# Seven block products instead of eight for the first layer's attention projections

## Chip, core and metric

One core of one Trainium2 chip. The time is the device time of one execution in microseconds; the median of the runs counts. All matrix work is fp32.

## What is computed

Two blocks after each other on 512 latent tokens (D = 1024) and 256 context tokens. The change is in the first block's first layer: both kinds of tokens are normed, modulated and projected, attended by three mixers of eight heads each (A: global, grouped keys, normed queries and keys, rotated; B: two-dimensional neighbourhood; C: window with a sink logit, rotated), gated with a silu and projected back.

```python
hx = rmsnorm(x, norm_w) * (1 + scale) + shift      # 512 tokens
hc = rmsnorm(cx, norm_w) * (1 + scale_c) + shift_c # 256 tokens
px = split_cols(hx @ w_in)    # qA kA vA qB kB vB qC kC vC gates
pc = split_cols(hc @ w_in)
ya, yca = global_gqa(...); yb, ycb = neighbourhood_attn(...); yc_, ycc = window_gqa(...)
ux = concatenate([ya, yb, yc_]) * silu(px[9])
x = x + gate * (ux @ w_out)
```

The second layer, then a block with a recurrent and a Hyena mixer, a convolution and two mixtures of 16 experts follow; they make up the time from 1457 us on (the second layer from 830) and the change leaves them as they are, but for where the second layer's weighted values go.

## The kernel before

Everything is kept transposed: features on the 128 partitions, tokens along the free dimension. HT (8 tiles of 128 features x 768 tokens) holds the normed input, XC the residual. Weights arrive in units of 1 MB in a ring of four slots (W), loaded by SyncE's queue as they come free. GpSimd only issues DMAs: rows for the modulation vectors (in_mod_rows) and the biases of the B heads, in an order sorted by step.

Attention runs in 12 pairs of heads, B0 to B3, A0 to A3, C0 to C3; a pair has six query tiles of 128 tokens in the first layer (four latent, two context), so 72 steps. schedule() writes one order of items, and every engine walks the same list and picks what is its own. A step n is: S (scores of the next tile into BIG), T (transposes of this tile's probabilities into PT, two banks), mod (modulation sums on VectorE, one or two), T2 (the rest of T for over eight tiles), E (exponentials of the next tile on ScalarE, maximum and scaling on VectorE), then projections of the next pair as filler, then O (weighted values). VectorE takes O's result, multiplies by the gate (SG) and writes U.

The projections of pair i lie in the steps of pair i - 1. inserted() lists them: "mm" items for keys, queries, values and gates, each output tile in two parts (512 and 256 tokens) of eight matmuls, summed in one of two PSUM banks PJ that are used in turn (next_pj); ScalarE copies keys, queries and (B) values out of it, and takes tanh of the gates straight from it (L1645), after which VectorE combines tanh and gate, again from PJ (L2049). For A and C values are made by tokens ("vt", 48 matmuls of 128 columns, once for A and once for C since four pairs share keys). In B the values are transposed after that ("v_tokens", L994) and copied by VectorE (L2177). norm_ (A) has a square, a sum over the partitions on TensorE, logarithm and exponential on ScalarE (L1672, L1676) and a multiplication on VectorE (L2065); rope_ (A, C) has a matmul (L1014) and three operations of VectorE (L2075 to L2079). O writes the PJ bank that isn't the current one, so it waits for that bank's reader. Where a step has no filler two matmuls are issued to keep the clock ("clock").

The output projection (720 to 830 us) already goes by seven block products (PRODUCTS, outputs_from_products), with sums of weights and tokens on VectorE.

Lines: L804 is the helper mm of all projections, L1042 to L1053 are S, L1068 is T, L1089 is O, L1692 the exponentials, L1703 the copies of PT, L1992 the modulation sums, L2092 and L2094 the scaling, L2190 and L2206 bias and maximum.

Of the kernel before, what the change touches and what calls it, by code (L numbers as in the profile page):

```python
# [17 lines left out]
P = 128  # L18
D = 1024
KT = D // P  # L20
# [73 lines left out]

def inserted(layer, i):


    kind, j = PAIRS[i]
# [29 lines left out]
def weight(item):  # L128

    what = item[0]  # L130
    if what == "mm":
        return 2 if item[3] == 0 else 1
    return {"vt": 0.5, "v_tokens": 2.5, "norm_k": 3, "norm_q": 3, "rope_k": 2, "rope_q": 2}[what]


def late_transposes(layer, i, t):
# [3 lines left out]
    return 2 * keys > 8  # L140


def schedule(layer):
# [6 lines left out]
    for i in range(1, len(PAIRS)):  # L150
        todo = inserted(layer, i)
# [11 lines left out]
    if layer == 0:  # L163
        order.insert(order.index(("mm", 0, "q", 0, 0)), ("vectors", 0))
    for n in range(-1, last + 1):
# [7 lines left out]
        if n >= 0 and late_transposes(layer, *steps[n]):  # L173
            if todo and todo[0][0] == "mm" and todo[0][4] < KT - 1 or todo and todo[0][0] == "vt":
                order.append(todo.pop(0))
# [16 lines left out]
def unit_order():  # L192

    first = [("ada", 0, u) for u in range(MOD_UNITS * FIRST_STEPS)]
    for layer in range(DEPTH):
        u = 0
        for item in schedule(layer)[1]:
            if item[0] == "mm" and item[2] in ("k", "q") and item[3:] == (0, 0):
# [17 lines left out]
class Count:  # L216
# [4 lines left out]
    def __init__(self):  # L221
        self.big = self.pt = self.units = 0
# [23 lines left out]
    def next_unit(self):  # L246
        self.units += 1
        return self.units - 1
# [5 lines left out]

    def next_o(self):

        return self.use_pj(1 - self.pj_bank)
# [32 lines left out]
def build(nc, A):  # L290
# [15 lines left out]
    with ExitStack() as ctx:  # L306
# [205 lines left out]
        gate_tanh = sem("gate_tanh")  # L512
        pj_filled = sem("pj_filled")
# [11 lines left out]
        o_filled = sem("o_filled")  # L525
        hidden_filled = sem("hidden_filled")
# [49 lines left out]
        out_stored = sem("out_stored")  # L576

# [161 lines left out]
        def _(pool):  # L739
# [29 lines left out]

            load_mod_vectors(0)  # L770
# [6 lines left out]
            jobs.append((mod_step(MODS_DONE[1] - 1), 2, 0))  # L777
            for _, what, x in sorted(jobs):
                if what == 0:
# [17 lines left out]
        def _(pe):  # L797
# [144 lines left out]
            def attention(layer):  # L942
# [4 lines left out]
                outputs, before_last = [0, 0], None  # L947
                if layer:
                    me.next("probs_exp", 2)
                kv = -1  # L950
                use = None
                for item in order:
                    what, x = item[0], item[1]
                    if what == "mm":
# [15 lines left out]
                        if k == KT - 1:  # L970
# [4 lines left out]
                            if which in ("v", "g") and b == (NA if which == "v" else nq):  # L975
                                unit_done()
                    elif what == "vt":
# [10 lines left out]
                    elif what == "v_tokens":  # L988
                        pe.wait_ge(pj_free[raw_use["v", x][0]], raw_use["v", x][1] + 1)
                        for tiles in (range(4), (4, 5, 6)):  # L990
                            use = next_pj()
                            for t in tiles:
                                token = NEAR_FROM[t] if t in NEAR_FROM else t * P
                                last = pe.transpose(PJ[use[0]][:, t % 4 * P:t % 4 * P + P],  # L994
                                                    SQT[:, token:token + P], const("ident"))
# [59 lines left out]
                    elif what in ("T", "T2"):  # L1055
                        i, t = steps[x]
                        tiles = prob_tiles(PAIRS[i][0], t)
                        for n, (h, y) in enumerate(tiles):
# [4 lines left out]
                            if n % 4 == 0:  # L1063
                                unit_at = me.next_unit()
                                if unit_at >= 2:
                                    pe.wait_ge(t_copied, unit_at - 1)
                            a = unit_at % 2 * 512 + n % 4 * P
# [4 lines left out]
                    elif what == "O":  # L1072
# [4 lines left out]
                        use_o = me.next_o()  # L1077
# [1730 lines left out]
```

## Time and profile before

| | us |
|---|---|
| runs | 3037.84, 3032.97, 3027.95 |
| median | 3032.97 |
| profiled execution, whole | 3034.02 |
| its span in the trace | 3032.2 |
| first layer's attention, steps of all pairs | 45 to 720 |
| its output projection | 720 to 830 |
| TensorE busy in the span | 2894.1 |
| VectorE busy | 1291.7 |
| ScalarE busy | 748.6 |
| GpSimd busy | 82.8 |

Times in the trace are microseconds from the span's start. A row of a timeline gives start, length, engine, line, operation and, in brackets, how long the engine idled before it and whose work ended that.

### The profile page before, as it was taken

The page shows a single profiled execution, that of the slowest core. Times are in us where ns is not written, and L with a number is a line of the kernel's source. Part 1 is how long each engine was busy: PE and PEld are TensorE (multiplying, and loading weights), DVE is VectorE, ACT ScalarE, POOL GpSimd, SP SyncE. Part 2 cuts the span into 40 slices and gives each one's busy share as a digit, 9 for nine tenths or more (in the row PEclk, how much of TensorE's full clock was granted, in tenths as well). Part 3 has the DMA queues.
Part 4 walks back from the last instruction along what each step waited for, and adds up shares of the span by engine and source line. Part 5 has one row for each costly group of instructions (what it writes and reads, how often), then busy time and mean ns, then how long its engine had stood idle before and what let it go on. Part 6 is the DMA issues. An engine that isn't in the chain of part 4 may idle for free.

```text
span 3032.2 us, 33976 instructions
## 1 busy us (share of the span) xinstructions
PE 2894.1 (95%) x13444; PEld 1538.4 (51%) x13444; DVE 1291.7 (43%) x2511; ACT 748.6 (25%) x1338; POOL 82.8 (3%) x156
## 2 busy tenths in 40 slices
PE   7999989999999999989999999999999998999998
PEld 3556656665555655558544545444443434444442
DVE  1455665787335466684466742111112533111112
ACT  3223455342122354340352111000002122000001
POOL 0000000000000000010000000000000000000000
PEclk9999999999999999999999999999999999999999
DMA  6222221223113233332111038999994225999997
GB/s 270 80 87 73 80 92 62 87 81 112 74 59 139 96 118 101 122 131 106 66 64 42 27 120 330 409 421 422 422 420 200 83 83 228 409 421 421 422 421 295
DMA packets 90526, 583.44 MB, mean 192 GB/s; under 512 B 10176, under 2 KB 10176, under 8 KB 29216
## 3 DMA queue, kind: packets, MB, share of 16 engines
q1 hardware_dynamic: 69696, 502.56, 41.3%
q0 software_dynamic: 20704, 79.11, 7.8%
q8 instruction: 90, 1.47, 0.2%
q14 instruction: 36, 0.29, 0.0%
HBM read 579.53 MB, written 2.10 MB: 192 GB/s over the span
## 4 chain that ended last, share of the span: by engine, by line
PE 86%; DVE 9%; ACT 3%; issue 1%; DMA 1%; SPq 0%; DVEq 0%; ACTq 0%
PE BIG L804 46%; PE PJ L804 20%; PE BIG L1535 4%; PE PT L1068 3%; PE PJ L1089 3%; PE BIG L1049 2%; PE BIG L1053 2%; PE PT L804 1%; DVE SPILL L1992 1%; PE PJ L853 1%; DVE STAT L2206 1%; ACT ARENA L1692 1%; PE BIG L1042 1%; PE PT L1511 1%; DMA W<-in_units 0%
## 5 line engine op out<-in xcount | busy, mean ns | idle before, releaser
L804 PE MATMUL PJ<-HT,W 128*128 128x512 f32 (+1 forms) x1792 | 649.8, 513 | 11.4 <-ACT ARENA L1672 6.3
L804 PE MATMUL BIG<-ARENA 128*64 128x512 f32 (+3 forms) x2656 | 550.5, 459 | 4.8 <-DVE ARENA L2508 2.5
L804 PEld LDWEIGHTS PJ<-HT,W 128*128 128x128 f32 x1792 | 332.2, 192 | 250.1 <-issue 217.9
L804 PEld LDWEIGHTS BIG<-ARENA 128*128 128x128 f32 (+1 forms) x2656 | 289.7, 167 | 252.4 <-issue 222.8
L804 PE MATMUL BIG<-HT,W 128*128 128x512 f32 (+1 forms) x768 | 320.0, 577 | 2.4 <-DVE ARENA L2343 2.1
L804 PE MATMUL BIG<-W,ARENA 128*64 128x512 f32 (+1 forms) x1280 | 282.0, 573 | 0.9 <-DVE ARENA L2389 0.9
L1703 ACT ACTIVATE ARENA<-PT 128x512 f32<-128x512 f32 (+1 forms) x264 | 144.4, 583 | 468.4 <-PE PT L1068 467.6
L2537 DVE SCALAR_TENSOR_TENSOR XC<-BIG,MOD,XC 128x512 f32<-128x512 f32 x128 | 90.2, 747 | 377.9 <-PE BIG L1535 377.9
L804 PEld LDWEIGHTS BIG<-HT,W 128*128 128x128 f32 x768 | 146.5, 191 | 172.9 <-issue 165.7
L1992 DVE CUSTOM_DVE_ANT_0 SPILL<-W,VEC 128x1024 bf16<-128x1024 f32 x168 | 214.8, 1278 | 11.2 <-issue 4.5
L2206 DVE TENSOR_REDUCE STAT<-BIG 128x1 f32<-128x512 f32 (+5 forms) x240 | 170.0, 725 | 46.8 <-PE BIG L1053 41.9
L804 PEld LDWEIGHTS BIG<-W,ARENA 128*64 128x64 f32 (+1 forms) x1280 | 107.4, 142 | 161.0 <-issue 154.8
L1692 ACT ACTIVATE ARENA<-BIG,STAT 128x512 f32<-128x512 f32 (+5 forms) x240 | 170.9, 717 | 21.5 <-DVE STAT L2206 20.7
L804 PE MATMUL BIG<-HT,ARENA 128*64 128x512 f32 x576 | 169.7, 592 | 0.0
L1089 PEld LDWEIGHTS PJ<-ARENA 128*64 128x64 f32 x2048 | 110.4, 136 | 92.8 <-issue 51.4
L1089 PE MATMUL PJ<-ARENA 128*64 128x128 f32 x2048 | 139.3, 278 | 18.2 <-DVE ARENA L2049 11.7
L1068 PE MATMUL PT<-CONST,ARENA 128*128 128x128 f32 x1024 | 148.6, 281 | 6.0 <-DVE ARENA L2094 4.3
L1068 PEld LDWEIGHTS PT<-CONST,ARENA 128*128 128x128 f32 x1024 | 111.8, 141 | 66.7 <-issue 44.1
L804 PE MATMUL BIG<-ARENA,W 128*128 128x512 f32 (+2 forms) x384 | 136.5, 513 | 0.1
L2094 DVE TENSOR_SCALAR ARENA<-ARENA,STAT 128x512 f32<-128x512 f32 (+3 forms) x240 | 121.6, 506 | 8.5
L2101 DVE SCALAR_TENSOR_TENSOR ARENA<-PJ,ARENA 128x128 f32<-128x128 f32 x120 | 37.4, 312 | 192.2 <-PE PJ L1089 191.7
L1535 PE MATMUL BIG<-ARENA 128*128 128x512 f32 x256 | 115.0, 602 | 0.0
(282 smaller groups left out, 2352.1 us busy)
## 6 DMA issues: line engine op xcount, KB each, us to landing
ARENA<-in_exp_w SPq DMA_DIRECT2D x168, 1024.0 KB, 18.1
W<-in_exp_w SPq DMA_DIRECT2D x144, 1024.0 KB, 16.8
W<-in_units SPq DMA_DIRECT2D x89, 1024.0 KB, 5.0
HT<-in_exp_w SPq DMA_DIRECT2D x72, 1024.0 KB, 22.0
W<-in_mod_rows POOLq DMA_DIRECT2D x128, 512.0 KB, 3.9
ARENA<-in_bias_b POOLq DMA_DIRECT2D x16, 384.0 KB, 5.5
XC<-in_x SPq DMA_DIRECT2D x1, 3072.0 KB, 11.2
W<-in_mod_vectors POOLq DMA_DIRECT2D x2, 1024.0 KB, 7.9
```

The source lines that it names most:

```text
L804: ins = pe.matmul(out, lhsT, rhs, start=start, stop=stop, skip_group_check=skip)
L1049: pe.matmul(BIG[h][:, N - (b - a) * P:N], Q[rows, i % 2, t * P:t * P + P], keys[rows, a * P:b * P], start=True, stop=True)
L1053: pe.matmul(BIG[h][:, N:NA], Q[rows, i % 2, t * P:t * P + P], keys[rows, N:NA], start=True, stop=True).then_inc(scores_filled, 1)
L1068: last = pe.transpose(PT[:, a:a + P], PROB[:, h, y * P:y * P + P], const("ident"))
L1089: last = pe.matmul(PJ[use_o[0]][head * HD:head * HD + HD, 0:P], V[:, buf_of[i], tile, head * HD:head * HD + HD], PTS[:, at:at + P], start= ...
L1535: last = pe.matmul(BIG[k_use % 2][:, half * N:half * N + N], YK[:, m * P:m * P + P], GSCAT[:, :], start=True, stop=True)
L1692: act.activation(PROB[:, h, 0:b - a], BIG[h][:, a:b], ACT.Exp, bias=STAT[:, c:c + 1], accum_out=STAT[:, 4 + c:5 + c]).then_inc(probs_exp, 1)
L1703: act.activation(PTS[:, a:a + w], PT[:, bank:bank + w], ACT.Copy).then_inc(t_copied, 1)
L1992: dve.tensor_tensor_reduce(SPILL[:, :], MODW[:, row % 2, :], MODV[:, which, :], 1.0, vec("mod_b", at), ALU.mult, ALU.add, MOD[:, at:at + 1 ...
L2094: dve.tensor_scalar(probs, probs, STAT[:, 8 + c:9 + c], None, ALU.mult)\
L2206: dve.tensor_reduce(STAT[:, c:c + 1], out[:, a:b], AX.X, ALU.max, negate=True).then_inc(max_ready, 1)
L2537: ins = dve.scalar_tensor_tensor(XC[:, m, 0:N], BIG[k_use % 2][:, half * N:half * N + N], mod(group, 5, m, 0), XC[:, m, 0:N], ALU.mult, AL ...
```

## The change

In the first layer all projections but the first pair's keys and values go in units of two output tiles (keys and values, or queries and gates) over all 768 tokens, by seven products of 2 x 2 blocks: features in halves of four tiles, tokens in halves of 384, the two output tiles as the other halves. A product is four matmuls of 384 columns into a PJ bank. Products 6, 7 and 4 go on adding in the bank of products 1, 6 and 7 (X), product 3 in that of product 5; products 1, 6, 5 and 4 are copied from there by ScalarE into their destination and products 2, 7 and 3 are added to it by VectorE.

- Four sums of weight blocks per unit are made on GpSimd, one in place over a block of the loaded weights; before each it waits for the unit's load and for the last product that reads the sum before. Four differences of token blocks are made once, on VectorE, in XC, and x is loaded into XC again behind the last unit.
- The gate is copied raw into SG, tanh goes over all 768 tokens at once from SG, and VectorE combines them in SG ("tanh", "gate" items).
- Values of A and C come out as features by tokens like those of B and are transposed ("v_tokens").
- The order of the items is new (inserted_by_blocks, block_slots): the "next" item puts what follows a step later; in the A and C pairs the last step's filler is the next unit's first product.
- Weighted values (O) go, in both layers, to the PT bank of the last transposes instead of a PJ bank, with a semaphore of their own (o_read) that the next transposes into that bank wait for.

Two steps where B0 ends and B1 begins, from the new schedule (P are products; x is a count of matmuls):

```
S5(B0 t5) | T 4 | mod 6 | mod 7 | E 5 | qg P3 x3 | qg P4 x4 | tanh 1 | O 4
S6(B1 t0) | T 5 | mod 8 | E 6 | gate 1 | v_tokens 1 | kv P1 x4 | kv P2 x4 | kv P6 x2 | O 5
```

The diff, cut to its core:

```diff
+BLOCK_PRODUCTS = [1, 2, 6, 5, 7, 3, 4]
+BLOCK_K = KT // 2
+BLOCK_N = NA // 2
+def inserted_by_blocks(i):
+    kind, j = PAIRS[i]
+    out = []
+    if i == 0:
+        out += [("mm", i, what, part, k) for what in ("k", "v") for part in range(2) for k in range(KT)]
+    elif kind == "B":
+        out += by_blocks(i, "kv")
+    elif kind == "A" and j == 0:
+        out += by_blocks(i, "kv", 0, 6) + [("square", i, "k")] + by_blocks(i, "kv", 6)
+        out += [("v_tokens", i), ("norm_k", i)]
+    elif j == 0:
+        out += by_blocks(i, "kv") + [("v_tokens", i)]
+    if kind == "A":
+        out += by_blocks(i, "qg", 0, 6) + [("square", i, "q")] + by_blocks(i, "qg", 6) + [("norm_q", i)]
+    else:
+        out += by_blocks(i, "qg")
+    out.append(("tanh", i))
+    if i == 0:
+        return out + [("v_tokens", i), ("gate", i)]
+    if j == 0 and kind != "B":
+        out.append(("rope_k", i))
+    return out + [("next", i)] + ([("gate", i), ("v_tokens", i)] if kind == "B" else [("rope_q", i), ("gate", i)])
...
+            def add_weights(u):
+                n, (a11, a12, a21, a22) = weights_of(u)
+                pool.wait_ge(unit_loaded[n % RING], 16 * (n // RING + 1))
+                if u:
+                    pool.wait_ge(pj_filled, uses[u - 1][3][0])
...
+                pool.tensor_tensor(ADDED[:, 0], a21, a22, ALU.add).then_inc(weights_added, 1)
+                pool.wait_ge(weights_added, 4 * u + 1)
+                pool.tensor_tensor(ADDED[:, 1], ADDED[:, 0], a11, ALU.add).then_inc(weights_added, 1)
+                pool.tensor_tensor(a21, a21, a11, ALU.add).then_inc(weights_added, 1)
+            def add_last_weights(u):
...
+                pool.tensor_tensor(ADDED[:, 2], ADDED[:, 1], a12, ALU.add).then_inc(weights_added, 1)
...
+                    pool.wait_ge(pj_filled, uses[-1][6][0])
+                    pool.dma_start(XC[:, :, :], A["x0"]).then_inc(x_again, 16)
...
+                        product = BLOCK_PRODUCTS[position]
+                        if k == 0:
+                            use = next_pj()
+                            if product in (6, 7, 3):
+                                pe.wait_ge(weights_added, 4 * block_unit + {6: 2, 7: 3, 3: 4}[product])
...
+                        last = mm(PJ[use[0]][:, 0:BLOCK_N], lhsT, rhs, k == 0 and product in (1, 2, 5),
+                                  k == BLOCK_K - 1, skip=product in (6, 7, 3, 4))
...
+                                if output_in[unit_at % 2]:
+                                    pe.wait_ge(o_read, output_in[unit_at % 2])
...
-                        use_o = me.next_o()
-                        if use_o[1]:
-                            pe.wait_ge(pj_free[use_o[0]], use_o[1])
...
+                        bank = (units_through[x] - 1) % 2
...
-                                last = pe.matmul(PJ[use_o[0]][head * HD:head * HD + HD, 0:P],
+                                last = pe.matmul(PT[head * HD:head * HD + HD, bank * 512:bank * 512 + P],
...
+                        act.wait_ge(pj_filled, use[2])
+                        scale = -1.0 if tile else block_scale(i, which)
+                        for out, src in block_parts(i, of, dst, PJ[use[0]], half):
+                            ins = act.activation(out, src, ACT.Copy, scale=scale)
+                        ins.then_inc(pj_free[use[0]], 1)
...
+                        if product in (2, 7):
+                            dve.wait_ge(pj_free[before[0]], before[1] + 1)
+                        dve.wait_ge(pj_filled, use[2])
+                        scale = -1.0 if tile else block_scale(i, which)
+                        for out, src in block_parts(i, of, dst, PJ[use[0]], half):
+                            ins = dve.scalar_tensor_tensor(out, src, scale, out, ALU.mult, ALU.add)
+                        ins.then_inc(pj_free[use[0]], 1)
+                    elif what == "gate":
+                        dve.wait_ge(gate_tanh, me.next("gate_tanh"))
+                        dve.scalar_tensor_tensor(SG[:, x % 2, :], GATE_T, 1.0, SG[:, x % 2, :],
+                                                 ALU.add, ALU.mult).then_inc(gated, 1)
```

## Rows read from the trace of the kernel before

**Rows 1.** The page's part 1: busy time, share, instructions.
```profile
PE 2894.1 (95%) x13444; PEld 1538.4 (51%) x13444; DVE 1291.7 (43%) x2511; ACT 748.6 (25%) x1338; POOL 82.8 (3%) x156
```

**Rows 2.** Busy time by stretch: engines' busy us (instructions), clock, DMA share, GB/s.
```profile
103.00:285.00 182.00, 176.08 (x894) 108.98 (x894) 94.03 (x214) 50.35 (x126) 10.20 (x19) 0.99 0.25 86
285.00:352.00 67.00, 63.14 (x384) 42.95 (x381) 38.03 (x79) 25.49 (x52) 3.26 (x6) 1.00 0.22 75
352.00:500.00 148.00, 134.33 (x817) 82.11 (x815) 90.17 (x184) 87.36 (x156) 8.79 (x16) 1.00 0.25 82
500.00:560.00 60.00, 58.17 (x389) 42.05 (x389) 31.55 (x66) 17.38 (x40) 2.15 (x4) 1.00 0.17 53
560.00:683.00 123.00, 118.51 (x717) 73.71 (x716) 103.32 (x269) 49.93 (x123) 7.43 (x14) 1.00 0.27 86
```

**Rows 3.** TensorE's waits from 45 to 720 us: total, times, longest.
```profile
PE BIG L1049 <- DVE ARENA L2079: 8.4, 7, 1.4
PE PJ L804 <- ACT ARENA L1672: 6.7, 4, 1.8
PE PJ L994 <- DVE ARENA L2049: 5.1, 4, 2.1
PE BIG L1042 <- DVE ARENA L2049: 2.2, 4, 1.0
```

**Rows 4.** The chain that ended last, pieces: start, us, what (512, 384, 256, 128 columns).
```profile
1770.85 6.87 PE PT L804 x16
725.13 23.46 PE BIG L804 x72
1368.90 15.54 PE BIG L804 x72
309.30 9.20 PE PJ L804 x80
```

**Rows 5.** Timeline of the step S6 (B1's first scores): TensorE's transposes, VectorE's chain.
```profile
155.42 0.66 PE L1068 MATMUL PT<-CONST,ARENA 128*128 128x128 f32 x4
155.50 0.43 DVE L2190 TENSOR_TENSOR BIG<-BIG,ARENA 128x256 f32<-128x256 f32 x1 [1.05 <-PE BIG L1053]
157.63 1.27 DVE L1992 CUSTOM_DVE_ANT_0 SPILL<-W,VEC 128x1024 bf16<-128x1024 f32 x1
159.62 0.49 DVE L2094 TENSOR_SCALAR ARENA<-ARENA,STAT 128x512 f32<-128x512 f32 x1
```

**Rows 6.** Timeline of VectorE: two value copies, a product over 768 columns.
```profile
86.83 1.28 DVE L2177 COPY ARENA<-PJ 128x512 f32<-128x512 f32 x2
387.20 1.02 DVE L2065 SCALAR_TENSOR_TENSOR ARENA<-ARENA,VEC 128x768 f32<-128x768 f32 x1 [3.15 <-ACT ARENA L1676]
```

**Rows 7.** Busy time by stretches of 4 us, columns as in rows 2.
```profile
144.00:148.00 4.00, 1.80 (x10) 0.85 (x8) 3.85 (x11) 1.20 (x5) 0.54 (x1) 1.00 0.13 28
148.00:152.00 4.00, 4.00 (x11) 3.23 (x12) 0.50 (x1) 0.00 (x0) 0.00 (x0) 0.57 0.27 103
2436.00:2440.00 4.00, 0.52 (x2) 0.00 (x0) 3.75 (x8) 0.00 (x0) 0.00 (x0) 0.86 1.01 426
2440.00:2444.00 4.00, 3.69 (x5) 1.62 (x6) 1.40 (x3) 0.42 (x1) 0.00 (x0) 0.50 0.11 45
```

**Rows 8.** Timeline of ScalarE in A0's last step: logarithm, exponential and their table loads.
```profile
382.66 1.28 ACT L1672 ACT_TABLE_LOAD   x1
385.03 1.28 ACT L1676 ACT_TABLE_LOAD   x1
387.19 1.28 ACT L1678 ACT_TABLE_LOAD   x1
```

**Rows 9.** Timeline around S54 (C1's first scores): VectorE's rotation, TensorE.
```profile
592.15 0.66 PE L1068 MATMUL PT<-CONST,ARENA 128*128 128x128 f32 x4
598.20 0.69 DVE L2079 TENSOR_TENSOR ARENA<-ARENA 128x512 f32<-128x512 f32 x1
```

**Rows 10.** TensorE's waits from 830 to 1365 us, the second layer.
```profile
PE PJ L1089 <- DVE ARENA L2049: 11.7, 8, 2.2
```

More of the change, by code:

```diff
@@ L92, in mod_step, with by_blocks, block_slots @@
     return late + x * (sum(STEPS) - SECOND_VECTORS - 1) // len(MOD_OPS)
+BLOCK_PRODUCTS = [1, 2, 6, 5, 7, 3, 4]
+BLOCK_K = KT // 2
+BLOCK_N = NA // 2
+def by_blocks(i, which, first=0, end=len(BLOCK_PRODUCTS)):
+    return [("block", i, which, position, k) for position in range(first, end) for k in range(BLOCK_K)]
+def inserted_by_blocks(i):
[20 more added lines that the diff above has]
+    return out + [("next", i)] + ([("gate", i), ("v_tokens", i)] if kind == "B" else [("rope_q", i), ("gate", i)])
+def block_slots(i, tiles):
+    todo = inserted_by_blocks(i)
+    early = BLOCK_K if PAIRS[i - 1][0] != "B" else 0
+    room = tiles if PAIRS[i][0] == "B" else tiles - 1
+    total, done, least, before = sum(weight(x) for x in todo[early:]), 0, 0, 0
+    out = [(-1, item) for item in todo[:early]]
+    for item in todo[early:]:
+        at = max(min(int(done * room / total), room - 1), least)
+        done += weight(item)
+        if item[0] == "next":
+            least = before + 1
+            continue
+        out.append((at, item))
+        before = at
+    return out
 def inserted(layer, i):
+    if layer == 0:
+        return inserted_by_blocks(i)
     kind, j = PAIRS[i]
@@ L132, in weight @@
         return 2 if item[3] == 0 else 1
-    return {"vt": 0.5, "v_tokens": 2.5, "norm_k": 3, "norm_q": 3, "rope_k": 2, "rope_q": 2}[what]
+    return {"block": 1.5, "square": 0, "tanh": 0, "gate": 0, "next": 0, "vt": 0.5, "v_tokens": 2.5, "norm_k": 3, "norm_q": 3, "rope_k": 2, "rope_q": 2}[what]
 def late_transposes(layer, i, t):
@@ L150, in schedule @@
     for i in range(1, len(PAIRS)):
+        if layer == 0:
+            for at, item in block_slots(i, tiles):
+                slots[(i - 1) * tiles - 1 + at].append(item)
+            continue
         todo = inserted(layer, i)
@@ L1092, in attention @@
                         last.then_inc(o_filled, 1)
-                for bank in range(2):
-                    pe.wait_ge(pj_free[bank], before_last[bank])
+                pe.wait_ge(o_read, steps_before + len(steps) - nq // P)
                 n = nq // 2
@@ L2036, in attention @@
                 kv = -1
+                use = None
+                if layer == 0:
+                    block_tokens()
                 for item in order:
@@ L2081, in attention @@
                         modulation(x)
+                    elif what in ("T", "T2"):
+                        columns = len(prob_tiles(PAIRS[steps[x][0]][0], steps[x][1])) * P
+                        me.next_unit(len([a for a in range(0, columns, 512) if (a < 1024) == (what == "T")]))
                     elif what == "S":
```

230 lines of the change are left out of this document (200 added, 30 removed).

## The prediction

> **What bounds the kernel now.** I read the page's totals first, then the busy time by stretch, then TensorE's waits, then the timelines of single steps. TensorE is busy 2894 of 3032 us, VectorE 1292 [rows 1]: time goes away only where TensorE's own work shrinks, and comes back wherever TensorE waits. The change touches the first layer's attention, 45 to 720 us. There TensorE works all but 6 us of 182 in the B pairs, 14 of 148 in the A pairs, 4.5 of 123 in the C pairs; but in C VectorE too is busy 103 of 123 [rows 2]. What TensorE waits for is a few hand-overs: rotated queries (L2079, 8.4 us), the norm's logarithm (L1672, 6.7), the gate's read before the value transposes (L2049, 5.1) [rows 3].
>
> **What a matmul costs.** Each fp32 matmul of the program is two rows of the trace (the x16 of a run of eight). Back to back one of 512 columns takes 6.87/8 = 0.86 us, of 384 23.46/36 = 0.65, of 256 15.54/36 = 0.43, and a value product of 128 columns 9.20/40 = 0.23 [rows 4]: proportional to columns down to 256.
>
> **The gain, on the path.** A unit (two output tiles over 768 tokens) is now 16 x 0.86 + 16 x 0.43 = 20.6 us; as seven products of four matmuls of 384 it is 28 x 0.645 = 18.06. Fifteen units gain 2.58 each: 38.7. The k/v units of A0 and C0 are now 10.3 + 48 x 0.23 = 21.4 and become 18.06 plus six transposes (four take 0.66 with their tail [rows 5], so about 0.8): 2.5 each, 5.0. Sum 43.7 us. The first k/v unit stays.
>
> **What it costs, step by step.** Two banks (PJ) now turn over every 2.6 us instead of 3.4 or more, and each product is read before the next but one may start. I walked each pair's order of steps with the durations of the rows: ScalarE's read comes behind the copies of the probabilities and the two exponentials, 2.2 to 2.7 us after the transposes end; VectorE's read behind the maximum, the modulation sums and the scaling, 4 us after them with one modulation sum, 5.3 with two. Most products are long enough to hide that. These aren't:
>
> (a) B1 to B3: the new order puts gate, then the two value copies, ahead of the next unit's first product, which uses the bank of the first copy. VectorE in that step: bias and maximum from 155.50, a modulation sum at 157.63, scaling until 160.11 [rows 5]. Behind that come the gate over 768 columns (1.02, by a norm's product of that size) and one copy (0.64) [rows 6]: the bank is free at 161.9. TensorE ends its four transposes at about 156.0 [rows 5] and seven value transposes at 156.9: it idles 5.0 us, and 6.4 in the two pairs with two modulation sums (1.35 more each). 17.8 us, in place of 5.3 of waits that go (most of L994's 5.1 and a part of L1042's 2.2 [rows 3]): 12.5. One product of B3's unit waits for VectorE's read behind two modulation sums: 0.7.
>
> (b) TensorE's clock. In 144 to 148 the engine idles 2.2 us, and the next 4 us have a granted clock of 0.57, i.e. mostly the lower of the two levels (1.2 GHz); after 3.5 us of idling at 2436 to 2440 it is 0.50 [rows 7]. Each such fall costs about 1.7 us of work. Three stalls of (a) bring three, and one of today goes: 3.4.
>
> (c) A0's own projections (in B3's steps): values wait for ScalarE's read (1.35), the norm for the value copy (1.1), a product for VectorE's read behind two modulation sums (2.6), the first scores of A0 for query rotation behind key rotation, maximum and two modulation sums (4.4), small ones 0.6: 10.1, against about 3.8 today (one wait each for the logarithm, the norm and the rotation, of those of rows 3), and two falls of the clock: 9.7.
>
> (d) A1 to A3: a gain. Today logarithm, exponential and tanh need table loads of 1.28 us, three of them in 6 us [rows 8], with TensorE waiting at both ends; with Tanh once after the norm the table loaded behind the square serves both, and norm and rotation are a step apart. I get 2.5 us of waits per pair against 4.5: -6.
>
> (e) C0's projections: 4.0 of waits against 1.0, one clock fall: 4.7.
>
> (f) C1 to C3: each step's rotation ends VectorE's chain 6.1 us after the transposes, whatever TensorE does [rows 9]: TensorE, with 0.86 us less work there, waits that longer (in the last pair 3.4). VectorE also gets three reads of about 0.55 and a gate of 1.02 per unit for gate reads of 0.68 and 0.42: 1.6 more, in a stretch where it is busy a third of 103, so 34.4 of 41 [rows 2]. Of 7.7 us saved I leave 1.5: 6.2.
>
> (g) The first unit: today's waits of 2.0 around its values shrink to 0.4: -1.6. Block sums of tokens are four VectorE operations of 1536 columns, 4 x 2.05 by the 1.35 ns a column of L2079 [rows 9]: 8.2 us, needed 20 us later, where VectorE has nothing else. Without that cover they would cost up to 8.
>
> (h) Weighted values go to PT: the wait of O for a PJ bank goes, also in the second layer, where it is 11.7 us [rows 10]. But next on TensorE are scores that need the rotation behind the same gate read, so it turns into that wait: -1, between 0 and -10.
>
> (i) The 68 weight sums on GpSimd. No row has one. By VectorE's 0.69 for 512 columns [rows 9] I take 0.7 as the lower end and 2.8 (four times that) as the upper. Four sums are at most 11 us per unit, with 12.9 us of products between the last use of a sum and its next: hidden, also the modulation rows' DMAs queued behind them on GpSimd, of which at least one is loaded ahead. What they do to VectorE: 0 to 40 us (below); I take 3, near the low end, since VectorE waits in more than half of the steps.
>
> (j) x is loaded again into XC (3 MB, 11 us at the start of the kernel) at about 660 us, needed at 720: nothing.
>
> Sum of costs: 12.5 + 0.7 + 3.4 + 9.7 - 6 + 4.7 + 6.2 - 1.6 - 1 + 3 = 31.6. Gain 43.7 - 31.6 = 12.1. The profiled execution took 3034.0 (span 3032.2), the median of three is 3033.0: forecast 3022.
>
> **The rule weighed.** What the rows show: VectorE's modulation sum, gate, norm and rotation read two SBUF operands each, and no row has GpSimd computing beside them. The Trainium skill, "SBUF — State Buffer", section "Who interferes with whom", says that a VectorE instruction with two SBUF inputs and a GpSimd one that reads SBUF exclude each other for the whole instruction. No row shows it. "GPSIMD Engine Reference", section 3.1, gives 2.6 cycles an element for such a sum, by which 512 elements would be an estimated 1.1 us and 68 of them 75 us, of which the shares of rival 2 would put an estimated 30 on the path.
>
> **The rivals.**
> Rival 1, the waits are smaller: if ScalarE and VectorE are as far ahead as in most steps of today, (a) is half, (c) and (e) don't grow and C keeps half its gain: 12.5 + 3.4 + 9.7 + 4.7 + 6.2 = 36.5 becomes 15, time 3000. For it: TensorE's present waits are only 38 us of 675. Against: the order of (a) is plain in the code.
> Rival 2, slower: GpSimd's sums hold VectorE up. Price: a sum of 0.7 to 2.8 us, 12 of them in C1 to C3 where VectorE is the bound, 16 in A0 and C0, 28 in units ahead of the gate and copies of (a). At 1.4 us, with all of the first, half of the second and a quarter of the third on the path: 17 + 11 + 10 = 38 in place of my 3: time 3057; it turns slower than before from about 0.5 us a sum on the path. For it: C's 84% VectorE. Against: 95 us of sums are a seventh of the stretch, and most operations of VectorE meet none.
> The rule of the Trainium skill's page "SBUF — State Buffer" is what rival 2 would rest on.
> Rival 3, the same: no contention, but C gains nothing, the clock falls at every new stall including the 2 us ones in C (six more, 1.7 each): 3022 + 1.5 + 10 = 3034.
> Rival 4, the products don't replace the work as said (a sum late for its product, so that TensorE waits for GpSimd in every unit, 2 us each): 3056.
>
> **How the numbers follow.** Forecast case (3012 to 3033) 0.48; rival 1 0.20; rival 2 0.15; rival 3 0.14; rival 4 0.03. A measurement of this kernel tells 0.3% (9 us) from no change. The forecast's case is split by that bound at 3023.9: 0.28 faster, 0.20 the same. Faster 0.48, same 0.20 + 0.14 = 0.34, slower 0.18. The range takes in rival 1 and half of rival 2: 2999 to 3048.
>
> **What would show it.** Right: PJ products with 384 columns at 0.645; a wait of L994's successor, the first product of B2, B3 and A0, for the value copy (L2177), 5 to 6.4 us, three times, with a granted clock of 0.5 behind it; a wait of A0's first scores for the rotation near 4 us; the waits for the logarithm in A1 to A3 gone; C pairs of 39 to 40 us instead of 41. Wrong: products waiting for GpSimd; VectorE operations of two SBUF operands longer or with gaps while GpSimd is busy; B pairs (60.5 us now) shorter than 58 or longer than 64.

## The result

| | before | after |
|---|---|---|
| median of 20 runs each, us | 3036.7 | 3039.2 |
| lowest to highest, us | 3028.0 to 3038.3 | 3036.1 to 3042.6 |
| ratio | 1 | 1.0016, 95% interval 1.0010 to 1.0022 |
| profiled execution: span, us | 3032.2 | 3040.8 |
| TensorE / VectorE / GpSimd busy, us | 2894 / 1292 / 83 | 2872 / 1343 / 176 |

The change makes the kernel slower by 5 us (0.16%), inside the 0.3% that counts as the same; forecast was 11 to 12 us less. The profiled execution of the changed kernel is the slowest of its 20 (3042.6), that of before lies under its median (3034.0), so the pair of traces is 8.6 us apart where the medians stand 2.5 and the ratio 4.9. The accounts below are made between the two traces, so up to some 4 us of their 8.6 are owed to which executions were traced. What differs between executions of one kernel is the granted clock: 31 executions of the kernel before run from 3027.7 us at a mean clock of 0.992 to 3039.0 at 0.988, and the 20 of the changed kernel from 3036.1 at 0.982 to 3042.6, the traced one, at 0.980.

TensorE's busy time by stretch, from its first projection to C3's first scores, first before, then after. Columns: stretch, length, busy us of TensorE, its weight loads, VectorE, ScalarE, GpSimd (instructions), granted clock, DMA share, GB/s. The borders are the first scores of B0, A0, A3, C0 and C3, as each trace has them, so that a wait for a pair's first scores counts in the stretch before.

```profile
44.30:92.83 48.53, 45.35 (x144) 26.29 (x145) 10.31 (x20) 16.96 (x27) 3.41 (x7) 0.95 0.32 125
92.83:342.86 250.03, 240.25 (x1270) 152.43 (x1269) 130.12 (x291) 75.06 (x176) 13.45 (x25) 0.99 0.24 83
342.86:491.54 148.68, 135.01 (x836) 82.99 (x834) 93.09 (x188) 83.48 (x153) 8.79 (x16) 1.00 0.25 82
491.54:558.33 66.79, 64.96 (x406) 44.87 (x404) 33.89 (x68) 24.14 (x47) 2.15 (x4) 1.00 0.20 64
558.33:680.30 121.97, 117.48 (x717) 73.54 (x716) 102.34 (x265) 48.97 (x120) 7.43 (x14) 1.00 0.27 87
```

```profile
44.30:88.47 44.17, 43.65 (x135) 25.07 (x137) 19.85 (x24) 17.04 (x28) 16.04 (x13) 0.93 0.32 124
88.47:348.79 260.32, 232.92 (x1155) 141.32 (x1153) 150.06 (x322) 80.19 (x192) 53.36 (x57) 0.94 0.25 83
348.79:483.99 135.20, 128.18 (x813) 79.28 (x811) 102.90 (x194) 73.47 (x147) 26.60 (x28) 0.99 0.28 90
483.99:556.55 72.56, 64.94 (x332) 39.30 (x330) 36.24 (x73) 25.85 (x50) 11.61 (x12) 0.93 0.14 47
556.55:688.33 131.78, 109.04 (x684) 67.98 (x683) 111.09 (x273) 51.29 (x122) 20.69 (x23) 0.96 0.30 103
```

What to see: 4.4 us go at the start, 10.3 come in B0 to B3, 13.5 go in A0 to A2, 5.8 come in A3, 9.8 come in C0 to C2. Where time comes in, two things changed beside the work: TensorE's idle part (27 of 260 us in B against 10 of 250) and its granted clock (0.93 to 0.96 against 0.99 to 1.00). From 720 us on both traces are the same but for the second layer's waits, which keep their sum.

TensorE's waits from 45 to 720 us, to be held against [rows 3] (total, times, longest):

```profile
PE BIG L1263 <- DVE ARENA L2373: 24.0, 8, 14.0
PE PJ L976 <- DVE ARENA L2477: 18.8, 4, 6.5
PE PJ L976 <- DVE ARENA L2344: 7.6, 4, 3.9
PE PT L1285 <- ACT ARENA L1959: 6.4, 12, 1.3
PE PJ L1208 <- ACT ARENA L1898: 3.4, 2, 2.2
```

L1263 are the first scores of a pair behind the rotation L2373, L976 the products behind the value copies (L2477) or VectorE's read (L2344), L1285 transposes, L1208 value transposes. In the same way L2391 below is VectorE's scaling of the probabilities and L2246 a modulation sum. The waits for the logarithm and the gate's read of [rows 3] are gone. One wait of 14.0 us stands at C3's first scores. The trace tells whose it is, in GpSimd's queue and on VectorE:

```profile
669.89 0.53 POOL L950 DMA_DIRECT2D XC<-in_x  x1 [10.53 <-PE PJ L976]
670.41 1.14 POOL L885 DMA_DIRECT2D W<-in_mod_rows  x2
...
683.12 1.28 DVE L2246 CUSTOM_DVE_ANT_0 SPILL<-W,VEC 128x1024 bf16<-128x1024 f32 x1 [10.50 <-DMA W<-in_mod_rows]
...
687.32 1.23 PE L1263 MATMUL BIG<-ARENA 64*128 64x256 f32 x4 [14.00 <-DVE ARENA L2373]
```

The reload of x (3 MB) is issued just ahead of the rows of the next two modulation sums. VectorE stands 10.5 us for those rows, and behind that sum come the scaling and the rotation that C3 needs.

### The profile page after: what moved, and what is told of

Read it like the earlier page. It is cut to its first block, busy times and chain, and to the rows that moved or that the text cites. A ratio compares the mean times of both kernels' runs of the same rounds, so it can differ in the third digit from the quotient of the medians.

```text
span 3040.8 us, 33707 instructions
## 1 busy us (share of the span) xinstructions
PE 2871.9 (94%) x13192; PEld 1513.9 (50%) x13192; DVE 1342.7 (44%) x2564; ACT 748.5 (25%) x1355; POOL 176.2 (6%) x225
## 3 DMA queue, kind: packets, MB, share of 16 engines
q8 instruction: 88, 1.44, 0.2%
## 4 chain that ended last, share of the span: by engine, by line
PE 68%; DVE 6%; ACT 1%; issue 1%; DVEq 0%; ACTq 0%
PE BIG L976 45%; PE PJ L976 9%; PE BIG L1748 4%; PE PT L1285 1%; PE PT L1302 1%; PE PT L976 1%; PE BIG L1263 1%; PE PJ L1025 1%; DVE SPILL L2246 1%; PE BIG L1267 1%; PE PT L1724 1%; DVE ARENA L2786 0%; DVE ARENA L2785 0%; PE BIG L1256 0%; PE PT L1704 0%
## 5 line engine op out<-in xcount | busy, mean ns | idle before, releaser
L976 PE MATMUL BIG<-ARENA 128*64 128x512 f32 (+3 forms) x2656 | 552.3, 461 | 4.8 <-DVE ARENA L2808 2.5
L976 PE MATMUL PJ<-HT,W 128*128 128x512 f32 (+2 forms) x1040 | 406.2, 541 | 26.2 <-DVE ARENA L2477 21.4
L976 PEld LDWEIGHTS BIG<-ARENA 128*128 128x128 f32 (+1 forms) x2656 | 290.2, 168 | 253.8 <-issue 224.2
L976 PE MATMUL BIG<-HT,W 128*128 128x512 f32 (+1 forms) x768 | 319.7, 577 | 2.4 <-DVE ARENA L2643 2.1
L976 PEld LDWEIGHTS PJ<-HT,W 128*128 128x128 f32 x1040 | 198.2, 197 | 191.1 <-issue 154.3
L976 PE MATMUL BIG<-W,ARENA 128*64 128x512 f32 (+1 forms) x1280 | 282.0, 573 | 0.9 <-DVE ARENA L2689 0.9
L976 PEld LDWEIGHTS BIG<-HT,W 128*128 128x128 f32 x768 | 146.2, 191 | 172.2 <-issue 164.8
L2246 DVE CUSTOM_DVE_ANT_0 SPILL<-W,VEC 128x1024 bf16<-128x1024 f32 x168 | 218.1, 1298 | 21.6 <-DMA W<-in_mod_rows 11.2
L976 PEld LDWEIGHTS BIG<-W,ARENA 128*64 128x64 f32 (+1 forms) x1280 | 107.4, 142 | 161.0 <-issue 154.9
L976 PE MATMUL BIG<-HT,ARENA 128*64 128x512 f32 x576 | 169.7, 592 | 0.0
L1285 PE MATMUL PT<-CONST,ARENA 128*128 128x128 f32 x1024 | 153.2, 286 | 14.1 <-ACT ARENA L1959 7.1
L1285 PEld LDWEIGHTS PT<-CONST,ARENA 128*128 128x128 f32 x1024 | 114.0, 143 | 76.8 <-issue 44.1
L1302 PEld LDWEIGHTS PT<-ARENA 128*64 128x64 f32 x2048 | 110.3, 136 | 70.5 <-issue 69.3
L2391 DVE TENSOR_SCALAR ARENA<-ARENA,STAT 128x512 f32<-128x512 f32 (+3 forms) x240 | 137.3, 572 | 8.5
L1302 PE MATMUL PT<-ARENA 128*64 128x128 f32 x2048 | 139.3, 278 | 0.0
L976 PE MATMUL BIG<-ARENA,W 128*128 128x512 f32 (+2 forms) x384 | 136.5, 513 | 0.1
L885 POOL DMA_DIRECT2D W<-in_mod_rows x128 | 69.1, 540 | 918.0 <-DVE MOD L2246 896.7
## 6 DMA issues: line engine op xcount, KB each, us to landing
XC<-in_x SPq DMA_DIRECT2D x1, 3072.0 KB, 10.1
```

Source lines behind the costliest of these rows:

```text
L885: pool.dma_start(MODW[:, x % 2, :], A["mod_rows"][x]).then_inc(mod_loaded[x % 2], 16)
L976: ins = pe.matmul(out, lhsT, rhs, start=start, stop=stop, skip_group_check=skip)
L1285: last = pe.transpose(PT[:, a:a + P], PROB[:, h, y * P:y * P + P], const("ident"))
L1302: last = pe.matmul(PT[head * HD:head * HD + HD, bank * 512:bank * 512 + P], V[:, buf_of[i], tile, head * HD:head * HD + HD], PTS[:, at:at ...
L2246: dve.tensor_tensor_reduce(SPILL[:, :], MODW[:, row % 2, :], MODV[:, which, :], 1.0, vec("mod_b", at), ALU.mult, ALU.add, MOD[:, at:at + 1 ...
L2391: dve.tensor_scalar(probs, probs, STAT[:, 8 + c:9 + c], None, ALU.mult)\
```

## The experiments

All are compared with the kernel before on the same chip. "Against the changed kernel" below is the difference of the two ratios times 3034 us; each ratio has an interval of some 0.1% to either side, so such a difference is good to 3 or 4 us; with three_mends and all_mends, of which only 5 and 4 executions were taken, to 5 or 6. Waits and clocks are from the traces and repeat to hundredths between kernels where nothing was touched (the wait for the first value copy is 5.03 or 5.04 in all six that leave it alone), so mechanisms are judged by them.

### x_on_sync and x_before_slot: another queue for the reload

```diff
-            jobs.append((uses[-1][6][1], 4, 0))
...
+            stream(A["units1"], last_block_unit + RING + 1, RING)
+            sp.wait_ge(pj_filled, block_uses()[-1][6][0])
+            sp.dma_start(XC[:, :, :], A["x0"]).then_inc(x_again, 16)
```

> The changed kernel with one edit: x is loaded again on SyncE's queue (behind the load that reuses the last unit's slot) instead of on GpSimd's, ahead of whose rows for the modulation vectors it stood. Theory: the 14.0 us wait of TensorE at C3's first scores is the queue's order (3 MB, 12 us, ahead of two rows DMAs): it falls to 3 to 5 us, and with it the low clock behind it (2.3 us lost): 10 to 13 us less than the changed kernel. Rival: the transfers share the DMA engines whatever the queue, the rows come as late: less than 4 us.

Measured: 1.0027 (1.0018 to 1.0035), nothing gained. C3's first scores wait 4.1 us, but the output products wait 12.3 for VectorE's first read into XC: the reload stood behind a load that itself waits for the first matmul of the output products, and so came late. That says nothing yet about the queues.

> The changed kernel with x loaded again on SyncE's queue, now ahead of the load that reuses the last unit's slot (that one waits for the output products' first matmul, and in x_on_sync the reload stood behind it, landed late and turned into a wait of 12.3 us there). Theory: C3's first scores wait 4.1 us as in x_on_sync instead of 14.0 and the output products wait for nothing: 10 to 12 us less than the changed kernel. Rival: on its own queue the reload slows the rows' transfers, and VectorE waits for them by 3 us or more around 675 to 685: 4 to 7 us less.

Measured: 1.0014 (1.0005 to 1.0023), 1 us less than the changed kernel. The reload is issued at 669.53 on SyncE's queue, the rows at 669.22 and 670.65 on GpSimd's. (x_before_slot puts the reload ahead of the load that it stood behind in x_on_sync, whose diff is shown.) TensorE waits 10.4 us instead of 14.0. VectorE in x_before_slot:

```profile
679.45 1.28 DVE L2246 CUSTOM_DVE_ANT_0 SPILL<-W,VEC 128x1024 bf16<-128x1024 f32 x1 [6.91 <-DMA W<-in_mod_rows]
```

Its DMA issues of 669 to 684 us (KB each, median us to landing):

```profile
XC<-in_x SPq DMA_DIRECT2D x1, 3072.0 KB, 11.4
W<-in_mod_rows POOLq DMA_DIRECT2D x3, 512.0 KB, 10.2
```

512 KB that land in 3.8 us elsewhere take 10.2 beside the 3 MB, though on a queue of their own. The theory fails, and the rival has the mechanism right: the order in one queue was 3.6 us of the wait, the sharing of the DMA engines the larger part (10.4 against the 4.1 that are left without the reload, below). The Trainium skill says this in "DMA: Bandwidth & Descriptors", section "Issuing engines are not separate DMA queues": transfers from any engine run on the same 16 engines and interleave. By that rule the trace agrees. The rival's size, 4 to 7 us less, isn't borne out: the time is 1 us less, good to 3.

### x_in_pieces: the reload between the rows

```diff
+            jobs += [(uses[-1][6][1] + 1 + k // 2, 4, k) for k in range(KT)]
...
+                    pool.dma_start(XC[:, x, :], A["x0"][:, x, :]).then_inc(x_again, 16)
```

> The changed kernel with the reload of x cut into eight DMAs of 384 KB, on GpSimd's queue as before, two in each of the four steps after the last block product, each behind the rows of its step. In x_before_slot the rows (issued 0.3 us ahead of the 3 MB and 1.1 us behind its start, on another queue) still came 6.9 us late for VectorE: not the queue's order alone but the shared transfers. Theory: rows wait for at most 3 us of other bytes, C3's first scores wait 3.5 to 4.6 us instead of 14.0: 9 to 12 us less than the changed kernel. Rival: the later rows come late in turn, one step each: 3 to 6 less.

Measured: 0.9989 (0.9980 to 0.9998), 8 us less than the changed kernel. The line of C3's first scores:

```profile
675.30 1.23 PE L1263 MATMUL BIG<-ARENA 64*128 64x256 f32 x4 [4.09 <-DVE ARENA L2373]
```

14.00 became 4.09, and the rival falls: from 650 to 745 us VectorE waits 1.2 us for rows, three times, at most 0.6, instead of 11.2. So the reload cost 9.9 us of wait; the other 4.1 are the rotation's.

### values_on_scalar: who copies the values of B

```diff
-                        values(kv, 0, me.next_pj())
...
+                                act.activation(V[:, kv % 2, a:b, :].rearrange("p a b -> p (a b)"),
+                                               PJ[use[0]][:, 0:(b - a) * P], ACT.Copy).then_inc(pj_free[use[0]], 1)
```

> The changed kernel with one edit: the two copies of the transposed values of B1 to B3 are made by ScalarE instead of VectorE. In the profile ScalarE is done with its exponentials 2.6, 4.0 and 4.0 us before VectorE's copy ends. Theory: the three waits for that copy (5.03, 6.36, 6.47 us) become 2.4 each, 10.6 us less, and with shorter stalls the clock comes back sooner, 1 to 3 us more: 11 to 14 us less than the changed kernel. Rival: VectorE is late for the next read anyway and the wait moves on to a product: 5 us or less.

Measured: 0.9973 (0.9962 to 0.9983), 13 us less than the changed kernel. The first of the three waits, in the changed kernel and here:

```profile
142.54 1.27 DVE L2246 CUSTOM_DVE_ANT_0 SPILL<-W,VEC 128x1024 bf16<-128x1024 f32 x1
...
144.93 0.95 DVE L2348 SCALAR_TENSOR_TENSOR ARENA<-ARENA 128x768 f32<-128x768 f32 x1
145.91 1.15 DVE L2477 COPY ARENA<-PJ 128x512 f32<-128x512 f32 x2
146.75 8.36 PE L976 MATMUL PJ<-HT,W 128*128 128x384 f32 x16 [5.03 <-DVE ARENA L2477]
```

```profile
142.02 0.97 ACT L1922 ACTIVATE ARENA<-PJ 128x512 f32<-128x512 f32 x2
142.75 3.06 PE L976 MATMUL PJ<-HT,W 128*128 128x384 f32 x5 [2.35 <-ACT ARENA L1922]
```

All three waits are 2.35 us (forecast 2.4), whether one or two modulation sums lie in the step: ScalarE doesn't stand behind them. The waits shrink by 10.8, the clock gives back the rest. No wait of another kind grew by more than 0.3 us.

### clock_kept: the same waits at full clock

```diff
+                            pe.wait_ge(t_copied, me.units)
+                            idle_bank({2: 5, 3: 7, 4: 7}[i], (me.units - 1) % 2)
...
+                        if layer == 0 and {24: 3, 66: 15}.get(x):
```

> The changed kernel with one addition: while TensorE waits for the value copies of B1 to B3, for A0's first scores and for C3's first scores it does matrix products of 512 columns into an idle PSUM bank (5, 7, 7, 3 and 15 of them, 0.86 us each at full clock, less than the wait they stand in). Theory: the granted clock of 0.50 behind these five waits costs 3.0, 2.1, 2.9, 1.2 and 2.3 us, 11.5 in all, and that is what goes: 8 to 12 us less than the changed kernel, with no wait shorter. Rival, that the low clock is covered by other waits or stays low: 0 to 3 us less, or more time.

Measured: 0.9985 (0.9977 to 0.9994), 9 us less than the changed kernel, with no wait made shorter by another engine. To see the clock's cost by itself I summed, over windows of 4 us from 44 to 740, TensorE's busy time times one less the granted clock: 3.8 us before, 21.8 in the changed kernel, 8.7 here. The windows behind the third value wait, in the changed kernel:

```profile
268.00:272.00 4.00, 0.00 (x0) 0.00 (x0) 3.78 (x9) 0.38 (x2) 0.55 (x1) 0.60 0.38 101
272.00:276.00 4.00, 2.87 (x5) 1.69 (x6) 1.42 (x3) 0.00 (x0) 0.00 (x0) 0.50 0.22 50
276.00:280.00 4.00, 4.00 (x9) 2.09 (x8) 0.00 (x0) 0.49 (x1) 0.00 (x0) 0.62 0.65 248
280.00:284.00 4.00, 4.00 (x14) 2.41 (x13) 0.56 (x1) 0.00 (x0) 0.00 (x0) 1.00 0.00 0
```

At 0.50, the lower level of 1.2 GHz, 2.87 us of busy time hold 1.4 us of work; this fall costs 1.44 + 1.52 = 3.0 us. The prediction had 1.7 for each. The trace of before could have told: it read the fall behind 3.5 us of idling only in the stretch 2440 to 2444 [rows 7], where it costs 1.8, and the stretch behind that one, in the kernel before, costs another 0.9:

```profile
2444.00:2448.00 4.00, 4.00 (x18) 1.45 (x17) 3.73 (x7) 4.00 (x8) 0.00 (x0) 0.78 0.00 0
```

### narrow_sums: the price of GpSimd's sums

```diff
+                n = slice(0, 1 if u else P)
+                pool.tensor_tensor(ADDED[:, 0, :, n], a21[:, :, n], a22[:, :, n], ALU.add).then_inc(weights_added, 1)
```

> The changed kernel with GpSimd's weight sums (from the second unit on) over one column of each 128 instead of all: left out is the rest of these sums, waits and order stay. It prices what GpSimd's work does to the others. Theory: VectorE's scaling of the probabilities goes back from 0.66-0.80 to 0.49-0.62 us (16 us in all over VectorE), of which a third is on the path: 3 to 7 us less than the changed kernel. Rival 2 of the prediction: some 38 us less. Rival, all of it hidden: under 2 us.

Measured: 0.9998 (0.9989 to 1.0007), 5.5 us less than the changed kernel, good to some 3. (Its trace is 9.2 us shorter, of which 2.8 are clock by the sum over windows, 19.0 instead of 21.8.) How it comes about, in A0's projections of the changed kernel (GpSimd, then VectorE), and the same two scalings with narrow sums:

```profile
289.46 1.45 POOL L919 TENSOR_TENSOR ARENA<-W 128x512 f32<-128x512 f32 x1 [19.84 <-PE PJ L976]
290.99 1.15 POOL L921 TENSOR_TENSOR ARENA<-ARENA,W 128x512 f32<-128x512 f32 x1
...
289.90 1.29 DVE L2391 TENSOR_SCALAR ARENA<-ARENA,STAT 128x512 f32<-128x512 f32 x1
291.30 1.13 DVE L2391 TENSOR_SCALAR ARENA<-ARENA,STAT 128x512 f32<-128x512 f32 x1
```

```profile
285.50 0.52 DVE L2393 TENSOR_SCALAR ARENA<-ARENA,STAT 128x512 f32<-128x512 f32 x1
286.12 0.49 DVE L2393 TENSOR_SCALAR ARENA<-ARENA,STAT 128x512 f32<-128x512 f32 x1
```

A scaling that falls on a sum ends just after it. Over the first layer (45 to 720 us) the scalings take 84.4 us in the changed kernel, 69.6 here and 69.4 before; modulation sums that begin behind a GpSimd sum take up to 2.20 us instead of 1.28, 128.7 against 127.8 in all (98 and 100 of them in the window). Reads from PSUM keep their 0.55 beside a running sum. Two instructions with two large SBUF operands each, the case of the prediction, meet too: in the first unit three of GpSimd's sums take 2.5 to 2.8 us beside VectorE's token sums, instead of 1.1 to 1.3. So the exclusion is there, and it costs VectorE some 18 us in scalings and modulation sums (14.8 in the scalings, 98 x 0.035 in the modulation sums), but only about a third of that reaches the end. The Trainium skill, "SBUF — State Buffer", section "Who interferes with whom", names this: tensor_scalar can use both port pairs of VectorE, and whichever of it and GpSimd issues first holds the shared one for the whole instruction. By that rule the trace agrees; the prediction had looked for it in instructions with two SBUF operands only, and most of the price (14.8 of 18 us) lies in scalings, which have one.

Where VectorE is the bound the price is plain: C0's steps take 40.08 us with narrow sums, 41.36 in the changed kernel and 41.15 before.

### vectors_earlier: a silu in the wrong step

```diff
-MODS_SECOND = 7 * 6 - 1
+MODS_SECOND = 7 * 6 - 2
```

> The changed kernel with the silu of the second modulation vectors (1.28 + 1.91 + 1.28 us on ScalarE with its two table loads) one step earlier than the first modulation sum that uses it. Theory: VectorE's wait of 4.49 us for it is what makes A3's product P5 wait 3.86: that goes, with 1.2 us of low clock: 4 to 5 us less than the changed kernel. Rival: ScalarE is then late for the exponentials or the read of P1 and a wait of 2 to 4 us stands a step earlier: within 1.5 us.

Measured: 1.0003 (0.9994 to 1.0012), 4 us less than the changed kernel; A3's steps go from 72.6 to 66.4 us. What stood there, in the changed kernel:

```profile
487.59 1.28 ACT L1967 ACT_TABLE_LOAD   x1
488.88 1.91 ACT L1967 ACTIVATE W<-W 128x2048 f32<-128x2048 f32 x1
490.81 1.28 ACT L1968 ACT_TABLE_LOAD   x1
...
490.92 1.28 DVE L2246 CUSTOM_DVE_ANT_0 SPILL<-W,VEC 128x1024 bf16<-128x1024 f32 x1 [4.49 <-issue]
...
494.19 4.46 PE L976 MATMUL PJ<-XC,ARENA 128*128 128x384 f32 x8 [3.86 <-DVE ARENA L2344]
```

In the kernel before VectorE waits the same 4.49 us at the same sum (at 498.48 there), and TensorE has enough projections issued not to notice. With a bank turning over every 2.6 us it does.

### mods_late: modulation sums behind the reads

```diff
+            order += [] if layer else mods
             order.append(("O", n))
```

> The changed kernel with the first layer's modulation sums moved behind the step's scaling and reads, ahead of the read of the weighted values (on VectorE; nothing else moves). It tests that 'behind one or two modulation sums' is what made the waits. Theory: the waits for value copies 5.03, 6.36, 6.47 become 3.7 each, those of products for VectorE's read (2.35 and 3.86) and A0's and C1's and C2's first scores (3.34, 2.10, 1.99) lose 1.3 to 2.6 each: 13 us, with less clock lost 15 to 18 us less than the changed kernel; the 14.0 at C3 turns into a wait of some 8 to 10 a step later. Rival: the maximum of the next step comes later by the same, and exponentials and transposes wait instead: 5 us less or none.

Measured: 1.0015 (1.0006 to 1.0023), the same as the changed kernel: a miss. The second and third value wait fall to 4.2 us, not 3.7, the first stays at 5.1, C1's and C2's rotation waits nearly go, but transposes now wait for VectorE's read of the weighted values (12.4 us in all instead of 0.8), A2's first scores wait 2.6 instead of 0.7, and the wait at C3 splits into 3.6 and 5.5. (Its traced execution is its fastest, 3033, so only waits are read from that trace.) VectorE's order isn't free to give: what a step's reads win, the next step's maximum and output read lose. The rival holds.

### outputs_in_pt: that part alone

```diff
-    if layer == 0:
-        return inserted_by_blocks(i)
```

(and with it the slots, sums and reload; the weighted values stay in PT.)

> The kernel before with one part of the change: weighted values go to PT in both layers, all projections as before. Theory (the prediction's step h): the 11.7 us wait of the second layer turns into a wait of the scores for the rotation: 0 to 2 us less than the kernel before. Rival: the wait really goes: 8 to 10 us less, and then the block products alone cost more than the comparison of the two kernels shows.

Measured: 1.0010 (1.0002 to 1.0019), 3 us more than before by the ratio; its trace is 1.4 us shorter than that of before. No gain in either, so the rival falls. The second layer's waits for the rotation are 16.3 us in 8; before they were 4.3 for the rotation and 11.7 for the bank [rows 10], together 16.0. In the first layer A0 to A2 take 1.8 us more in all and C2 0.9 less. The A pairs' waits are 14.8 us in all, as before (14.9), but gathered into fewer and longer ones: three of 2.88 us for the logarithm, where before none in these pairs was over 1.8. Behind two of the three the clock falls, 2.8 us in all, and in these pairs of the kernel before it doesn't fall at all. How the 4.9 us of the whole change are split between this part and the block products lies within the intervals and stays open.

### two_mends, three_mends, all_mends: do the causes add up

Edits: two_mends is x_before_slot with values_on_scalar; three_mends is values_on_scalar, x_in_pieces and vectors_earlier; all_mends adds matrix products into an idle PSUM bank in the waits that are left:

```diff
+CLOCK_AT = {(2, 'kv', 1): 2, (3, 'kv', 1): 2, (4, 'kv', 1): 2, (4, 'qg', 5): 2}
...
+                        if layer == 0 and {24: 3, 54: 2, 60: 2, 66: 3}.get(x):
```

> x_before_slot and values_on_scalar together. Theory: the two are independent (12.4 us less by values_on_scalar, 10 to 12 by the reload): 21 to 25 us less than the changed kernel, about 3016. Rival: VectorE in between is the common bound, the gains overlap: 14 to 18.

Measured: 0.9970 (0.9958 to 0.9981), 14 us less than the changed kernel: the sum of 13 and of the 1 that x_before_slot brings, whose own expectation had been wrong.

> values_on_scalar, x_in_pieces and vectors_earlier together. Theory: they are independent, 12.4 + 10 + 4.5 less than the changed kernel: 27, or 0.9925 to 0.9945 of the kernel before. Rival: overlap on VectorE, 0.996 to 0.998.

Measured: 0.9929 (0.9915 to 0.9943), 26 us less than the changed kernel; 13 + 8 + 4 = 25. The rival's 0.996 to 0.998 lies outside the interval: within what these ratios can tell the three causes add up.

> three_mends with matrix products into an idle PSUM bank in the waits that are left (2 of 512 columns in each of the waits of 2.35, of 2.1 and 2.0 and of 2.19 us, 3 in those of 3.3 and 3.5 to 4). Theory: the low clock behind waits of 2 to 4 us (1.3 to 2.5 us a time in the traces so far, some ten times) goes: 8 to 11 us less than three_mends. Rival: behind waits of about 2 us the clock stays up by itself in most of them: 3 to 5 us.

Measured: 0.9891 (0.9875 to 0.9906), 3001.0 us: 11.5 us less than three_mends and 33 us less than the kernel before. Summed as above the low clock takes 3.0 us of the first layer, against 15.6 in three_mends, 12.6 less, so the rival's 3 to 5 us fall; half of what is left is at the start, half behind two waits of 1.0 and 1.2 us in A0's projections that weren't filled. Two products of a unit, at full clock (16 rows are 8 matmuls):

```profile
491.14 5.40 PE L977 MATMUL PJ<-HT,W 128*128 128x384 f32 x16 [0.95 <-DVE ARENA L2504]
```

With its tail 5.40 us, by the prediction's 0.645 a matmul 5.16. The saved work is there; what the changed kernel lacked was work of other engines done in time, and TensorE's clock behind the waits for it.

## Why the prediction was wrong

Forecast was 12.1 us less, the traces show 8.6 more: 20.7 us. The 3039 us lie within the range on record, 2999 to 3048, but only since it was wide: the kernel got slower, and what was missed, steps (j), (b), (c), (e) and (i) below, all went the same way. By stretch, forecast (summed from its steps) and measured, in us. The early first products count in: the first product of each A and C unit lies one pair ahead of where it was, which puts 2.6 us into B3 and takes 2.6 from C2 without saving anything.

| stretch | forecast | measured |
|---|---|---|
| start to B0's first scores | -4.2 | -4.4 |
| B0 to B3 | +8.3 | +10.3 |
| A0 to A2 | -13.7 | -13.5 |
| A3 | -0.4 | +5.8 |
| C0 to C2 | -4.1 | +9.8 |
| C3 | 0 | +0.5 |
| sums on GpSimd (3) and O in PT (-1), not placed | +2 | in the others |

**Right.** The saved work: TensorE's busy time, less what the low clock adds to it (summed over windows of 4 us as above, here over the whole span: 22.8 us before, 41.4 after), falls from 2871.3 to 2830.5, 40.8 us of the 43.7 forecast. Step (a): idle 5.0, 6.4, 6.4 forecast, 5.03, 6.36, 6.47 measured. Step (d): the stretch A0 to A2 comes within 0.2 us; the waits for the logarithm are gone. Step (g): the start gains 4.4 us, 4.2 forecast; the token sums take 10.2 us instead of 8.2 but are hidden. Step (h): the second layer's wait turned into the rotation's, its sum unchanged (16.2 for 16.0). In (c), A0's first scores wait 3.3 (4.4 forecast), the product behind two modulation sums 2.35 (2.6), the value transposes 1.2 (1.35), the norm 1.0 (1.1); together 8.1 with the rest, of 10.1.

**Wrong, step (j), 9.9 us.** "x is loaded again ...: nothing." The transfer itself was checked against its own deadline (720 us), not against what shares the DMA engines with it. Two modulation rows are queued behind it, and C3's rotation behind the sums that need them; neither was named. x_in_pieces takes it away (14.00 to 4.09). With the clock's fall behind it, counted in the next paragraph, it cost 12 us.

**Wrong in size, steps (b), (c), (e): the clock, 9 us.** Each fall was priced 1.7 us, from single stretches of 4 us in the kernel before. Behind the three value waits it cost 2.7, 2.2 and 3.0; after A3's two waits 1.2 and 2.9; three falls instead of two in A0's projections, 4.2 in all; and C3's wait brought one of 2.3 that follows from (j). In all 21.8 us where the forecast comes to 12.3 (3.8 of today and 3.4 + 3.4 + 1.7 of the steps). The 1.7 came from a short wait, of 2.15 us: behind the three of 2.35 us in values_on_scalar the falls cost 1.3, 1.5 and 1.4. Over all traces with the waits of 5.0 to 6.5 us unfilled they cost 1.1 to 3.0 behind them, 2.3 on average, so the changed kernel's trace, its slowest execution, stands in the upper part of that. After waits of 2.0 and 2.1 us (C1, C2) the clock fell in some traces (the C1 steps take 42.98 us in x_on_sync) and not in others (41.29 in the changed kernel). That executions of one kernel differ by their mean clock is on record (0.992 to 0.988 over the kernel before's 11 us); in which places they differ isn't, since one execution of each was traced.

**Wrong, step (e), 3 us.** Waits of 7.0 us for C0's projections instead of 4.0. Among them are the 3.86 that vectors_earlier takes away, and no step of the prediction names their cause: the silu of the second modulation vectors stands in A3's first step, and VectorE's modulation sum there begins only after a wait of 4.49 us, which the trace of before shows.

**Short, step (i), 2.5 us.** 5.5 instead of 3 (good to some 3, so this miss alone isn't clear of noise), on the side of rival 2 but a seventh of its 38. The sums themselves, 1.1 to 1.3 us undisturbed and 94 us in all, came as rival 2 had them; its groups of 12, 16 and 28 leave out the 12 of A1 to A3. The rival had the mechanism right; its shares for the path were far too high, since VectorE's lengthened scalings mostly eat time that it would have idled in.

**Step (f)** left 1.5 us of gain in C1 to C3. C0 and C1 lose 0.2 and 0.3 each instead; with narrow sums they gain 1.1 and 0.2 against before (C1 in spite of a fall of the clock), so it is GpSimd that took it. The last pair's own wait, 4.1, was forecast as 3.4.

These make 9.9 + 0.7 + 9.5 + 3.0 + 2.5 = 25.6 against 20.7. 2.0 of the difference is what (c) had too much; 2.9 stay open, within what adding a ratio's 5.5 to lengths of traces can tell.

Of the rivals, 3 (more clock falls and no gain in C, 3034) came nearest in place and size, though C's loss came from GpSimd and the reload; the reload was in no rival. Rival 4 didn't occur: no product waits for GpSimd.

## What to carry over

When a saving shortens the work between two hand-overs, the waits that were covered before set the price: list every instruction with a wait of its own in the steps around it (here a silu with two table loads, a value copy behind a modulation sum) and give each hand-over to the engine that is free first. Check a bulk reload not against its own deadline only but against every small transfer that is due while it runs, and cut it to fit between them. Price a wait of TensorE with the lower clock seen behind waits of about its own length, followed until the clock is back at 1.00; matrix products into an idle PSUM bank during the waits got back 12.6 us of the 15.6 that it cost in three_mends.

## What the runs showed of the hardware

- Two queues, one set of DMA engines: 512 KB land in 3.8 us in the kernel before, in 10.2 us beside 3 MB on another queue (x_before_slot).
- GpSimd's sums of two fp32 operands over 128 x 512 take 1.1 to 1.3 us undisturbed and up to 2.8 where they meet VectorE; a tensor_scalar of VectorE over 512 columns takes 0.49 us, up to 1.59 beside one, though it reads only one large SBUF operand.
- The granted clock fell behind every unfilled wait of 3.3 us and more, behind most of those of 2.2 to 2.4 and some of those of 2.0 to 2.1. What a fall cost, over all traces: 1.1 to 1.7 us behind waits of 2.35 to 3.9 (once 2.7, behind 3.86 us in clock_kept), 1.4 to 3.1 where one of 0.95 follows one of 2.19 (A3), 1.7 to 2.6 behind those of 4.0 to 4.2, 1.1 to 3.0 behind those of 5.0 to 6.5, 1.9 to 2.5 behind those of 10 to 14, and next to nothing where the wait was filled with matrix products.
